# Two attention heads in one step, on the two halves of TensorE's rows, with the products beside them taken by halves of the tokens

## The reference, cut to what matters

```python
def chunked_rel_attention(q, k, v, rel_bias):      # CHUNK = 64, LEFT_CHUNKS = 8, head width 64, 8 heads
    ...
    scores = jnp.einsum('bnqhd,bnkhd->bnhqk', qc, kb).astype(jnp.float32) * (dh ** -0.5)
    scores = scores + bias[None, None]
    scores = jnp.where(valid[None, :, None, None, :], scores, jnp.float32(-1e30))
    p = jax.nn.softmax(scores, axis=-1).astype(v.dtype)
    out = jnp.einsum('bnhqk,bnkhd->bnqhd', p, vb)
    return out.reshape(b, s, h * dh)

def second_block(...):
        n = rms_norm(x, mix_norm_g[l])
        proj = jnp.einsum('bsd,de->bse', n, w_in[l])
        q, k, v, bg, cg, xh, su, sv = jnp.split(proj, cuts, axis=-1)
        y_a = chunked_rel_attention(q.reshape(shp), k.reshape(shp), v.reshape(shp), rel_bias[l])
        y_b = gated_short_conv(bg, cg, xh, conv_w[l])
        y_c = spatial_gating(su, sv, sg_ln_g[l], sg_ln_b[l], sg_w[l], sg_b[l])
        mixed = jnp.concatenate([y_a, y_b, y_c], axis=-1)
        g = group_norm_g[l].reshape(N_GROUPS, GROUP_DIM)
        mixed = rms_norm(mixed.reshape(b, s, N_GROUPS, GROUP_DIM), g).reshape(b, s, MIX_WIDTH)
        x = x + jnp.einsum('bse,ed->bsd', mixed, w_out[l])
```

## Time and profile before

| what | us |
|---|---|
| median of 3 executions | 3756.25 |
| the profiled execution | 3751.47 |
| its span | 3750.2 |
| TensorE busy | 3675.1 (98%) |
| VectorE busy | 1740.7 (46%) |
| ScalarE busy | 1176.5 (31%) |
| GpSimd busy | 1094.2 (29%) |
| first scores (L858) at | 1423.8 |
| last outcome transposed (L895) at | 1714.2 |

### The profile page before, as it was taken

One profiled execution on the slowest core, in us unless ns is written; L12 is line 12 of the kernel. 1 busy time (PEld: TensorE's weight loads), 2 busy tenths in 40 slices (PEclk: granted clock), 3 DMA queues, 4 the chain that ended last, 5 costly groups with the idle time before them and its releaser, 6 DMA issues.

```text
span 3750.2 us, 42170 instructions
## 1 busy us (share of the span) xinstructions
PE 3675.1 (98%) x17644; PEld 3006.4 (80%) x17644; DVE 1740.7 (46%) x2140; ACT 1176.5 (31%) x1523; POOL 1094.2 (29%) x747
## 2 busy tenths in 40 slices
PE   7999999999999999999999999999999999999998
PEld 6999987888888877777888888877777788888886
DVE  6676616999643472225432222227666642222226
ACT  5555522222231444453321111114322331211113
POOL 4333411222233441012432222225113442222223
PEclk9999999999999999999999999999999999999999
DMA  2100121111242331001311111114112221111112
GB/s 104 34 29 29 34 85 40 57 57 51 84 152 90 104 123 34 33 30 40 113 62 45 51 45 51 46 45 132 40 34 79 62 73 46 45 46 51 45 51 73
DMA packets 65132, 229.29 MB, mean 61 GB/s; under 512 B 7216, under 2 KB 7472, under 8 KB 64944
## 3 DMA queue, kind: packets, MB, share of 16 engines
q1 hardware_dynamic: 64944, 226.60, 18.3%
HBM read 201.40 MB, written 25.17 MB: 60 GB/s over the span
## 4 chain that ended last, share of the span: by engine, by line
PE 90%; DVE 7%; issue 2%; ACT 1%; POOL 0%; DMA 0%; SPq 0%; DVEq 0%; ACTq 0%
PE psum L508 78%; PE psum L858 2%; PE psum L620 2%; PE psum L873 2%; PE psum L888 1%; PE psum L591 1%; DVE fb L2106 0%; PE psum L744 0%; PE psum L706 0%; PE psum L644 0%; PE psum L643 0%; DVE hl L2037 0%; DVE pb L2879 0%; DVE Ab L2141 0%; DVE k L2845 0%
## 5 line engine op out<-in xcount | busy, mean ns | idle before, releaser
L3137 POOL TENSOR_TENSOR wl<-raw,wh 128x512 fp32r<-128x512 f32 x636 | 884.3, 1411 | 2344.9 <-ACT wh L1189 2344.9
L508 PE MATMUL psum<-hh,wh 128*128 128x512 f32 (+2 forms) x3760 | 1180.9, 390 | 29.9 <-POOL wl L3137 9.2
L508 PE MATMUL psum<-hh,wl 128*128 128x512 f32 (+2 forms) x3760 | 1146.1, 380 | 0.0
L508 PE MATMUL psum<-hl,wh 128*128 128x512 f32 (+2 forms) x3760 | 1142.4, 379 | 0.0
L508 PEld LDWEIGHTS psum<-hh,wh 128*128 128x128 f32 x3760 | 673.5, 190 | 175.7 <-issue 32.1
L508 PEld LDWEIGHTS psum<-hh,wl 128*128 128x128 f32 x3760 | 696.1, 189 | 133.2
L508 PEld LDWEIGHTS psum<-hl,wh 128*128 128x128 f32 x3760 | 695.9, 189 | 131.9
L1189 ACT ACTIVATE wh<-raw 128x1024 fp32r<-128x1024 f32 x318 | 335.1, 1054 | 771.5 <-PE psum L508 769.1
L508 PE MATMUL psum<-hdh,wh 128*128 128x512 f32 x1024 | 334.1, 398 | 5.0 <-DVE B L3038 4.4
L508 PE MATMUL psum<-hdl,wh 128*128 128x512 f32 x1024 | 331.3, 396 | 0.0
L508 PE MATMUL psum<-hdh,wl 128*128 128x512 f32 x1024 | 331.2, 396 | 0.0
(11 more groups left out here) (423 smaller groups left out, 3035.9 us busy)
## 6 DMA issues: line engine op xcount, KB each, us to landing
raw<-in_wts SPq DMA_DIRECT2D x318, 512.0 KB, 3.6
keep_x<-B SPq DMA_DIRECT2D x14, 512.0 KB, 5.7
X<-in_xin SPq DMA_DIRECT2D x8, 520.0 KB, 5.3
keep_sz<-tmp SPq DMA_DIRECT2D x8, 512.0 KB, 2.9
tmp<-keep_sz SPq DMA_DIRECT2D x8, 512.0 KB, 3.9
av<-keep_gr SPq DMA_DIRECT2D x8, 512.0 KB, 3.2
av<-keep_gc SPq DMA_DIRECT2D x8, 512.0 KB, 3.7
xc<-keep_x SPq DMA_DIRECT2D x8, 512.0 KB, 5.6
```

Source lines behind the costliest of these rows:

```text
L508: ins = pe.matmul(out, w, x[:, k, c0:c0 + width], start=first and n == 0, stop=final and n == 2)
L3137: gp.tensor_tensor(wl[:, s, a], raw[:, s, a], fp(wh[:, s, a]), SUB).then_inc(*c.lo.tick(i, p))
```

## The change

Both heads of a pair are taken in one step n = 0 to 7. The scores of the two heads are issued in chunks of 256 keys, head 0 and head 1 in turn, to different rows of the array and to different banks (banks 0-1 for head 0, 4-5 for head 1). A step is four turns: scores of step n; transposes of step n - 1, both heads; product with v of step n - 2, head 0; the same, head 1. The slabs beside it give up banks 0-1: `gemm_halves` goes through the 8 steps k for one half of the tokens into bank 2, then for the other into bank 3, and takes a side turn after every 3 matmuls, so there are 48 turns beside three slabs. ScalarE evicts each half by itself (512 columns); the tile copied by DVE for keys 384 to 640 of head 1 is new. The division by the sums and the normalization are joined: DVE copies each step's outcome from PSUM, takes sums of squares of 64 channels, and once per pair forms `ss + 64 EPS rsum^2`, whose root's reciprocal scales all 1024 columns. The biases of a pair are loaded in SP's own order, before the third slab. For j = 0 the slabs QKV to QKV+2 stay as they were; beside the short convolution the slabs SHORT to SHORT+3 go by halves.

Removed lines of the attention functions (all shown above) and the scalar and vector engines' slab loops (evictions by halves, `slab_halves`: `split`, 9 turns, evict half 0, 7 turns, evict half 1) are left out of the diff.

```diff
@@ -372,14 +372,18 @@
     selB4 = C("selB4", 8).rearrange("p (t m) -> p t m", t=4)
     pairs = Banks([psum[:, 0:2, :], psum[:, 2:4, :]])
+    lanes = Banks([psum[:, 2, :], psum[:, 3, :]])
     head = Banks([psum[:, 4, :]])
     aux = Banks([psum[:, 5, :], psum[:, 6, :], psum[:, 7, :]])
-    S, TL, PT, OUT = psum[:, 4:6, :], psum[:, 5, 128:256], psum[:, 6, :], psum[:, 7, :]
+    S = [flat(psum[:, 4 * hd:4 * hd + 2, :]) for hd in range(2)]
+    OUT = S[1][:, 640:768]
+    PT = [flat(psum[:, 6:8, :])[:, 0:640], flat(psum[:, 6:8, :])[:, 640:1024], S[0][:, 640:896]]
     LB, OML = lbv[:, 1, :], lbv[:, 2, :]
     i_, f_, a_, u_, w_ = row[:, 0, :], row[:, 1, :], pb[0:4, 0, :], pb[0:4, 1, :], h3[0:4, :]
     shf = kd3[0:4, :]
...
-    def pp_slot(j, n):
-        return pp[:, (16 * j + n) % 3, :]
-    def pt_slot(j, n):
-        return pt[:, (16 * j + n) % 2, :]
+    def pp_slot(n, hd):
+        z = 2 * (n % 2) + hd
+        return pp[:, z, :] if z < 3 else flat(vg[:, :, :])[:, 0:BAND]
+    def pt_slot(n, hd):
+        a = BAND * (1 + hd)
+        return flat(vg[:, :, :])[:, a:a + BAND] if n % 2 else pt[:, hd, :]
...
+    def turned(n, hd):
+        return min(384, keys(n)[0]) if hd else keys(n)[0]
...
+        def gemm_halves(i, untils):
+            for hf in range(2):
+                grab(lanes, (i, hf), untils[hf])
+                for k in range(KT):
+                    ins = three(psum[:, 2:4, :], None, i, k, k, k == 0, k == KT - 1, hh, hl, META, (hf,))
+                    if k < KT - 1:
+                        side.turn()
+                ins.then_inc(*(c.gemm.tick(i, 0) if hf else c.gemm.tick(i, "left")))
+                side.turn()
...
         def attention(j):
             s = j % 2
...
             pe.wait_ge(*c.ev("av", j))
             for n in range(8):
...
+                ins = pe.transpose(S[1][:, n * 128:(n + 1) * 128], va[:, s, n * 128:(n + 1) * 128], ident)
             ins.then_inc(*c.at_pe.tick("vT", j))
             yield
...
+            for n in range(10):
+                if n < 8:
                     nk, k0 = keys(n)
...
                     if n == 0:
                         pe.wait_ge(*c.at_act("vT", j))
+                        if j:
+                            pe.wait_ge(*c.at_act("mx", j - 1))
                     else:
...
+                        pe.wait_ge(*(c.at_dve("o", j, n - 3) if n > 2 else c.at_dve("max", j, n - 1, 1)))
+                    for a0 in range(0, nk, 256):
+                        wd = min(256, nk - a0)
+                        for hd in range(2):
+                            lo = 64 * hd
+                            ins = pe.matmul(S[hd][:, a0:a0 + wd], qa[lo:lo + 64, s, n * 128:(n + 1) * 128],
+                                            ka[lo:lo + 64, s, k0 + a0:k0 + a0 + wd], start=True, stop=True)
                     ins.then_inc(*c.at_pe.tick("qk", j, n))
...
+                yield
+                if 1 <= n < 9:
                     m = n - 1
...
+                    nk = keys(m)[0]
                     if m:
...
+                        pe.wait_ge(*c.at_act("pT", j, m - 1, 1))
+                    for hd in range(2):
+                        pe.wait_ge(*c.at_act("exp", j, m, hd))
+                        for b_ in range(nk // 128):
+                            x, z = (PT[2], b_ - 3) if hd and b_ > 2 else (PT[hd], b_)
+                            if hd and b_ == 3:
+                                pe.wait_ge(*(c.at_dve("max", j, n, 0) if n < 8 else c.at_dve("pT", j, 6)))
+                            ins = pe.transpose(x[:, z * 128:(z + 1) * 128],
+                                               pp_slot(m, hd)[:, b_ * 128:(b_ + 1) * 128], ident)
                     ins.then_inc(*c.at_pe.tick("pT", j, m))
                 yield
...
+                for hd in range(2):
+                    if n >= 2:
+                        m = n - 2
+                        nk, k0 = keys(m)
+                        pe.wait_ge(*c.at_act("pT", j, m, hd))
+                        if hd == 0:
+                            if n < 8:
+                                pe.wait_ge(*c.at_dve("max", j, n, 1))
+                            elif m:
+                                pe.wait_ge(*c.at_dve("o", j, m - 1))
+                        elif nk > 384:
+                            pe.wait_ge(*c.at_dve("pT", j, m))
+                        for b_ in range(nk // 128):
+                            a0 = k0 + b_ * 128 + 64 * hd
+                            ins = pe.matmul(OUT[:, 64 * hd:64 * hd + 64], pt_slot(m, hd)[:, b_ * 128:(b_ + 1) * 128],
+                                            va[:, s, a0:a0 + 64], start=(b_ == 0), stop=(b_ == nk // 128 - 1))
+                        if hd:
+                            ins.then_inc(*c.at_pe.tick("pv", j, m))
+                    yield
+            yield from pause(4)
+            pe.wait_ge(*c.at_dve("tn", j))
             for i in range(8):
...
+                ins = pe.transpose(S[0][:, i * 128:(i + 1) * 128], oa[:, i, :], ident)
             ins.then_inc(*c.at_pe.tick("mx", j))
         job = None
@@ -904,13 +930,17 @@
                 side.drain()
                 job = side.add(spatial())
         for j in range(4):
-            gemm(QKV + 3 * j, c.ev("aq", j))
-            gemm(QKV + 3 * j + 1, c.ev("ak", j))
-            gemm(QKV + 3 * j + 2, c.ev("av", j))
+            for n, name in enumerate(("aq", "ak", "av")):
+                if j:
+                    gemm_halves(QKV + 3 * j + n, [c.ev(name, j, 0), c.ev(name, j)])
+                else:
+                    gemm(QKV + n, c.ev(name, 0))
             side.finish(job)
             if j == 0:
                 for point in aux.freed:
                     pe.wait_ge(*point)
+                lanes.freed = [c.ev("ak", 0), c.ev("ak", 0)]
+                assert pairs.n % 2 == 1
             job = side.add(attention(j))
         def tile_norm(m):
@@ -919,11 +949,17 @@
         for m in range(2):
             i = SHORT + 3 * m
-            gemm(i, c.ev("cg", m))
-            gemm(i + 1, c.ev_v("xh", m))
-            gemm(i + 2, c.ev("bg", m), last=(m == 1))
+            gemm_halves(i, [c.ev("cg", m, 0), c.ev("cg", m)])
             if m == 0:
+                gemm_halves(i + 1, [c.ev_v("xh", m, 0), c.ev_v("xh", m)])
+                gemm_halves(i + 2, [c.ev("bg", m, 0), c.ev("bg", m)])
+                side.finish(job)
                 side.add(tile_norm(0))
+            else:
+                pairs.only(psum[:, 0:2, :], psum[:, 2:4, :])
+                pairs.freed = [c.at_act("mx", 3), c.ev("cg", 1)]
+                gemm(i + 1, c.ev_v("xh", m))
+                gemm(i + 2, c.ev("bg", m), last=True)
         side.drain()
         side.add(pause(1))
         side.add(tile_norm(1))
...
@@ -1577,41 +1613,41 @@
         def attention(j):
             s = j % 2
...
             se.wait_ge(*c.at_pe("vT", j))
...
+            se.activation(va[:, s, :], S[1], COPY).then_inc(*c.at_act.tick("vT", j))
+            yield
+            for n in range(10):
                 yield
...
+                for hd in range(2):
+                    if n < 8:
+                        p = pp_slot(n, hd)[:, 0:keys(n)[0]]
+                        se.wait_ge(*c.at_dve("nm", j, n, hd))
+                        se.activation(p, p, EXP, bias=st2[:, 2 * (n % 2) + hd, 1:2],
+                                      accum_out=rsum[:, 2 * n + hd:2 * n + hd + 1]).then_inc(*c.at_act.tick("exp", j, n, hd))
+                    yield
+                if 1 <= n < 9:
+                    se.wait_ge(*c.at_pe("pT", j, n - 1))
+                    for hd in range(2):
+                        w = turned(n - 1, hd)
+                        se.activation(pt_slot(n - 1, hd)[:, 0:w], PT[hd][:, 0:w],
+                                      COPY).then_inc(*c.at_act.tick("pT", j, n - 1, hd))
+                yield
+            se.wait_ge(*c.at_dve("s", j))
+            se.activation(ss2[:, :], ss2[:, :], SQRT, scale=1.0 / 64).then_inc(*c.at_act.tick("ss", j))
...
+        def heads_of(ap):
+            return ap.rearrange("p t (h d) -> p (t h) d", h=2)
         def attention(j):
...
+            yield
+            for n in range(10):
+                if n < 8:
+                    nk = keys(n)[0]
+                    for hd in range(2):
+                        slot = 2 * (n % 2) + hd
+                        mx, nm = (st2[:, slot, z:z + 1] for z in range(2))
+                        if n == 0:
+                            ve.wait_ge(*c.loaded("bias", 2 * j + hd))
+                        if n >= 2:
+                            ve.wait_ge(*c.at_pe("pT", j, n - 2))
+                        elif j:
+                            ve.wait_ge(*c.at_pe("pT", j - 1, 6 + n))
+                        ve.wait_ge(*c.at_pe("qk", j, n))
+                        ve.tensor_tensor_reduce(pp_slot(n, hd)[:, 0:nk], S[hd][:, 0:nk], bias[:, hd, BAND - nk:BAND],
+                                                1.0, -3.0e38, ADD, MAX, mx).then_inc(*c.at_dve.tick("max", j, n, hd))
```

(82 more changed lines are left out.)

176 lines of the change are left out of this document (35 added, 141 removed).

## The result

The kernel after takes 3724.3 us (median of 4 runs, 3724.08 to 3726.73); the kernel before took 3757.06 us beside it (4 runs, 3752.93 to 3759.53). The ratio is 0.9915, with a 95% interval of 0.9898 to 0.9933: faster by 0.85%. The forecast was 3726. The profiled execution after took 3724.08 us with a span of 3722.8; before it was 3751.47 with 3750.2. So the spans differ by 27.4 us, where the prediction's sum made 29.8.

What follows compares the result with a forecast made beforehand. TensorE's own instruction stream was taken as the bound. Stream -34.6, waits +3.2, last pair -2.4 and norm +4.0 make -29.8 us, so 3756.25 becomes 3726 us (chance 0.62), range 3719 to 3743.

Steps and rivals of the forecast that it cites:

- Streaming: Scores on TensorE: the two heads' passes run at once on two row halves, streaming falls by 25.6 us.
- Fixed cost: Scores on TensorE: the fixed cost is paid 32 times, not 64, 9.0 us less.
- the moved turns: Product with v in turns of its own between slab products: costs nothing, bound 5.8 us.
- Waits at pair starts: TensorE waits for the halved slab eviction and the copy of v back: 3.2 us in sum.
- Waits within a step: TensorE's waits for DVE's reading of scores and copy of the outcome: covered, cost nothing, but covers thin.
- The last pair: Beside the convolution's taps, which delay DVE: TensorE's idle time falls from some 2.8 to 0.4 us, saving 2.4.
- `tile_norm(0)`: Norm with less cover between its turns: 1.0 us more at the sums, 3.0 at the spreading, together 4.0.
- A: Scores' passes keep strict order, one stands alone at each step's start and end: 6.3 us less saved, 3733; chance 0.14.
- B: Scores: the row halves don't run at once, all 25.6 us stay: 3752; chance 0.07.
- C: Waits within a step: the thin covers don't hold, half a microsecond per step: 3742; chance 0.11.
- D: As B, and each change of row half exposes a load of weights, 15.8 us more: 3768, slower; chance 0.06.

Runs made afterwards that it cites:

- The scores one turn apart: Kernel after, with head 1's scores issued one turn later than head 0's, slab products between them: 3764.52 us, ratio 1.0019.
- one-head-after-the-other kernel: Kernel after, with all chunks of head 0's scores issued first, then all of head 1's: 3737.33 us, ratio 0.9951.
- same-rows kernel: Kernel after, with both heads' scores computed from rows 0-63, instructions, chunks, banks and waits the same: 3753.06 us, ratio 0.9992.

## Why the prediction was right

- **Streaming, -25.6: right.** The step of 640 keys takes 1.28 us for 1.27 forecast, and taking the concurrency away costs 25.8 up to the norm. The step that decided was a transfer from the earlier trace rows: column halves stood for row halves, which no row of before showed, and they turned out to behave alike.
- **Fixed cost, -9.0, and the moved turns, nothing: right.** A pair lasts 65.53 to 65.59 us for 65.6 forecast (73.55 before). Up to the norm the sum of all terms was -33.8, measured -33.96. Without the 25.8 of streaming and the 2.3 saved at the last pair, and with the 2.9 of new waits made good, 8.8 are left for the fixed cost and the moved turns together. The scores one turn apart give 0.35 us per excursion.
- **Waits at pair starts, +3.2: right, slightly high.** By starts they are 0.57 for the first pair, 0.15 for each of the other three, and 0.48 four times: 2.94 us. The last falls to 0.20 when the copy is shared, so its cause is shown.
- **Waits within a step, nothing: right.** At least 0.28 and 0.34 us lie between the end of DVE's work and TensorE's start, where a start that waits comes 0.05 to 0.14 us behind.
- **The last pair, -2.4: right.** 0.45 us of idle time for 0.4 forecast, 2.3 saved.
- **`tile_norm(0)`, +4.0: the mis-sized term, measured +6.2.** Its idle times were forecast well: 0.96 us more for 1.0 at the sums, 2.82 for 3.0 at the spreading. What the step left out is that TensorE runs slower after such an idle time. The spreading's 3.0 is 5.2 in fact, as the kernel that removes only its wait shows. This is nearly the whole error of the sum, 27.6 or 27.4 against 29.8.
- **Rivals.** A gave 1.48 us for a step of 640 keys, measured 1.28; the one-head-after-the-other kernel shows passes starting ahead of ones issued earlier. B is the same-rows kernel: forecast 3752, measured 3753. C fell with the covers, whose ends are now in the trace. D needed exposed loads at each change of the row half; the couples 6 to 7 ns apart exclude them.

That the total came nearer (3724.3 for 3726) than the sum (27.4 for 29.8) is luck. The forecast was shifted by the 4.8 us that the profiled execution before lay under its median; the one after lies only 0.2 under its own. This error and that of the sum point opposite ways and nearly cancel.

## What to carry over

Matmuls of 64 contraction rows use half the array; put two independent ones on the two halves, in different banks, and issue them alternately. With four passes of one head ahead of the other's nothing was lost here, with six half of the overlap (1.82 us between 1.28 and 2.36). When a change shortens the work between two turns of TensorE's order, every chain of other engines that was hidden between them has to be priced again, also chains that the change doesn't name; here a norm far from the attention gave back 6.2 of 34 us, and a later turn recovered it. Read the granted clock behind each new idle time of TensorE: the waits at the spreading, 2.8 us, cost 2.4 us more here, because the work behind started at 1.2 GHz.

## What was not expected of the hardware

- Matmul passes on one half of the rows start ahead of passes on the other half that were issued earlier (1532.715 before 1532.821), but only from the third pass of the first head on, when the one that overtakes stood four places behind it in the order of issue. With four passes a head the two heads' passes start 13 ns apart from the first on.
- About an idle time of 2.1 to 2.3 us between matmuls the granted clock fell to 1.2 GHz, in one trace 0.4 us into it, in another 0.9 us after its end. In the kernel after TensorE then worked at the low clock for 5.1 us and lost 2.4 us. The idle times of 0.3 to 1.64 us from 1424 to 1694 us brought no fall: the clock's mean over them is 1.00.
- Copies of 128x512 from the two banks of one pair by ScalarE (0.60 us) and DVE (0.69 us) at the same time: ScalarE's took no longer than alone (0.60 at 1486.65).
